# A two-layer decoder step on one core: dense blocks of sample scores, second-layer index keys issued from three queues, page steps at tiles 10 to 44

## What is computed

```
z = rmsnorm(x) @ w_in                                   # 1024 -> 12 pieces: q k v qi ki wi gates, pool, gating
# sample rows: an indexer scores all old keys, 256 of them are attended
score = sum_h relu(qi_h . ki) * wi_h                    # ki: index keys of the pages, 64 wide
idx   = top_k(score, 256)
att   = softmax(q . k[idx]) @ v[idx]                    # k, v: pages of the cache, 512 wide
# prompt rows: the same with their own keys, top 128, causal; besides a pooling and a gating branch
x = x + rmsnorm(concat(branches * silu(gates)) @ w_out)
```

## Time and profile before

| | |
|---|---|
| median of 3 runs | 1106.1 us (1105.05 to 1114.48) |
| the profiled execution's own time | 1108.4 us |
| its span in the trace | 1106.7 us |
| PE busy | 985.8 us, 89% |
| DVE busy | 513.4 us, 46% |
| ACT busy | 322.7 us, 29% |
| pages and index keys, weights and the rest | 205 MB, 185 GB/s on average |

### The profile page before, as it was taken

The page is one execution under the profiler, slowest core; times in us unless marked ns, Lnnn a source line. Parts: engine busy times, 40 slices in busy tenths (PEclk is TensorE's granted clock), DMA queues, the critical chain, the costliest instruction groups (busy, mean ns, idle before and its releaser), DMA issues.

```text
span 1106.7 us, 18204 instructions
## 1 busy us (share of the span) xinstructions
PE 985.8 (89%) x5948; PEld 496.0 (45%) x5948; DVE 513.4 (46%) x1682; ACT 322.7 (29%) x718; POOL 89.3 (8%) x152
## 2 busy tenths in 40 slices
PE   5999987898989999999882999798989899999995
PEld 4534443343434555554451344343434345555542
DVE  4215999335972333232231069983349722332222
ACT  3132312421232544341210321233212324453411
POOL 8300000000000002002110000010000000020000
PEclk9999998898989999999987999998989899999998
DMA  9732657246674847456453224665475746465560
GB/s 299 184 108 77 237 202 286 93 171 237 206 251 157 281 144 256 162 186 216 133 155 111 79 77 154 231 225 208 146 263 173 276 164 247 153 232 192 177 232 29
DMA packets 110019, 205.01 MB, mean 185 GB/s; under 512 B 14439, under 2 KB 29014, under 8 KB 109938
## 3 DMA queue, kind: packets, MB, share of 16 engines
q1 hardware_dynamic: 87186, 141.86, 38.1%
q0 software_dynamic: 17632, 59.99, 15.7%
q10 hardware_dynamic: 5120, 2.10, 0.8%
HBM read 193.87 MB, written 10.14 MB: 184 GB/s over the span
## 4 chain that ended last, share of the span: by engine, by line
PE 60%; DVE 15%; SPq 9%; DMA 8%; issue 4%; ACT 2%; POOL 0%; ACTq 0%; POOLq 0%; DVEq 0%
PE bank L1355 27%; PE bank L1682 9%; DVE r L1006 6%; PE bank L1407 5%; SPq L559 5%; DMA pg<-in_cache_v_dram 3%; DMA pg<-in_cache_k_dram 3%; PE bank L1372 3%; SPq L591 3%; PE bank L1339 2%; PE bank L1611 2%; DMA r<-in_selectors_dram 2%; PE bank L1619 2%; PE bank L1505 2%; PE bank L1575 1%
## 5 line engine op out<-in xcount | busy, mean ns | idle before, releaser
L1355 PE MATMUL bank<-wr,ht 128*128 128x512 f32 (+1 forms) x1024 | 446.8, 591 | 0.9 <-issue 0.6
L1355 PEld LDWEIGHTS bank<-wr,ht 128*128 128x128 f32 x1024 | 194.7, 195 | 222.8 <-issue 208.7
L1006 DVE TENSOR_SCALAR_CACHE_REDUCE r<-r,sel_i 128x1088 bf16<-128x1088 f32 x62 | 82.8, 1335 | 0.0
L1407 PE MATMUL bank<-pg,rs 128*32 128x256 f32 x1024 | 67.0, 401 | 11.7 <-DMA pg<-in_cache_v_dram 11.7
L1339 PE MATMUL bank<-wr,ht 128*64 128x256 f32 (+1 forms) x576 | 68.3, 393 | 5.9 <-ACT r L937 3.4
L1372 PE MATMUL bank<-pg,qbx 128*32 128x256 f32 x1024 | 64.3, 388 | 9.0 <-DMA pg<-in_cache_k_dram 8.0
L1102 DVE CUSTOM_DVE_ANT_0 r<-bank,r 128x256 f32<-128x256 f32 (+2 forms) x48 | 24.9, 555 | 82.1 <-PE bank L1611 82.0
L1682 PE MATMUL bank<-wr,qt 128*128 128x512 f32 x128 | 60.1, 613 | 0.6 <-ACT r L937 0.6
L1682 PE MATMUL bank<-wr,ht 128*128 128x512 f32 x128 | 57.5, 592 | 0.0
L1339 PEld LDWEIGHTS bank<-wr,ht 128*64 128x64 f32 x576 | 42.8, 146 | 28.3 <-ACT r L937 5.1
L1268 DVE MATCH_REPLACE8 r<-m,r 128x256 f32<-128x256 f32 (+2 forms) x96 | 51.1, 542 | 0.0
(11 more groups left out here) (264 smaller groups left out, 1127.8 us busy)
## 6 DMA issues: line engine op xcount, KB each, us to landing
pg<-in_cache_k_dram SPq DMA_DIRECT2D x256, 256.0 KB, 4.3
pg<-in_cache_v_dram SPq DMA_DIRECT2D x256, 256.0 KB, 4.5
wr<-in_w_in_dram POOLq DMA_DIRECT2D x14, 2048.0 KB, 10.0
wr<-in_w_out_dram POOLq DMA_DIRECT2D x4, 2048.0 KB, 9.7
sh<-in_cache_kidx_dram SPq DMA_DIRECT2D x96, 32.0 KB, 4.4
r<-in_x_prompt_dram SPq DMA_DIRECT2D x4, 512.0 KB, 7.0
wr<-in_w_in_dram POOLq DMA_DIRECT2D x2, 1024.0 KB, 9.9
gr<-in_cache_kidx_dram ACTq DMA_DIRECT2D x64, 32.0 KB, 2.6
```

The lines of the kernel that those rows point to most:

```text
L1006: then(nc.vector.tensor_scalar(MSK, SC, scalar, None, ALU.is_ge, ALU.add, accum_out=CNT))
L1355: mm = pe.matmul(b[0:m, 0:w], HT[:, k, rt * P:rt * P + m], W[n % 2][:, k, 0:w], start=(k == 0), stop=(k == KC - 1))
L1407: mm = pe.matmul(acc[r0:r0 + 32, :], RS[n % 2][:, c0:c0 + 32], PG[2 * gi + e][:, g * DP:(g + 1) * DP], start=(j == 0 and u == 0 and e == 0 ...
```

## The change

- `S` and `H` stand in two dense blocks. The first, at the end of tile 7 (second layer: 6), holds `S(0, *)`, `kip`, `H(0)` and `S(1, *)` with no tile between them; the second, a tile later, holds `H(1)`, `S(2, *)`, `wt`, `sgus`, `H(2)`. The search starts there, two tiles earlier in the list.
- One relu of each step stays on ACT, the other goes to DVE, with a semaphore of its own (`s_free1`).
- In the second layer POOL issues the 32 odd keys of pairs 2 and 3 (`pool keys`), between tile 45 and tile 0 of the next layer. SP issues 64 in place of 96.
- The sample tiles of `kg` and `qi` stand at 2 and 3 in the second layer (4 and 5 before), that of `q` at 8 in both (10 before). `T` of `q` and `k` stands two tiles behind its tile in place of one.
- The page steps start at tile 10 in place of 12 and leave out 17, 22 and 27 in place of 15 and 21; the last is at 44 in place of 45. The masks of the first two pairs are split: three pieces at the end of tiles 17 and 18, two pieces, maximum and exponential at the front of 18 and 19.
- The store of the new rows to `x_mid` is issued by ACT in `norm`, ahead of its square, and no longer by POOL.

```diff
 KEY_STEPS = [("keys", 1, pair, j) for pair in (0, 1) for j in range(NCH)]
-
-PLACES = [12, 13, 14, 16, 17, 18, 19, 20, 22, 23, 24, 25] + list(range(26, 46))
+POOL_KEYS = [("pool keys", 1, pair, j) for pair in (2, 3) for j in range(NCH)]
+
+PLACES = [10, 11, 12, 13, 14, 15, 16, 18, 19, 20, 21, 23, 24, 25, 26, 28] + list(range(29, 45))
 PI_PLACES = [(n, part) for n in (18, 19, 20, 21, 22, 23) for part in (0, 2)]
...
-    tiles = [("z", l, "kg", rt) for rt in (RTO if l == 0 else RTP)]
-    tiles[1 if l == 0 else 5:1 if l == 0 else 5] = [("z", l, "qi", ST)]
-    tiles += [("z", l, "qi", rt) for rt in range(PT_TILES)]
-    for name in ("q", "k", "v"):
+    tiles = [("z", l, "kg", rt) for rt in range(PT_TILES)]
+    first = 0 if l == 0 else 2
+    tiles[first:first] = [("z", l, "kg", ST), ("z", l, "qi", ST)]
+    tiles += [("z", l, "qi", 0), ("z", l, "qi", 1), ("z", l, "q", ST), ("z", l, "qi", 2), ("z", l, "qi", 3)]
+    tiles += [("z", l, "q", rt) for rt in range(PT_TILES)]
+    for name in ("k", "v"):
         tiles += [("z", l, name, rt) for rt in RTO]
...
+        put(0, END, POOL_KEYS[7][:1] + POOL_KEYS[7][2:])
...
-    put(9, FRONT, ("kip",))
...
     s0 = 7 if l == 0 else 6
-    put(s0, MID, *[("S", 0, p) for p in range(PAIRS)])
-    put(s0 + 1, MID, ("H", 0), *[("S", 1, p) for p in range(PAIRS)])
-    put(s0 + 2, MID, ("H", 1), *[("S", 2, p) for p in range(PAIRS)])
-    put(s0 + 3, FRONT, ("H", 2))
-    put(s0 + 3, MID, ("wt",))
-    put(s0 + 4, MID, ("sgus",))
+    put(s0, END, *[("S", 0, p) for p in range(PAIRS)], ("kip",), ("H", 0), *[("S", 1, p) for p in range(PAIRS)])
+    put(s0 + 1, END, ("H", 1), *[("S", 2, p) for p in range(PAIRS)], ("wt",), ("sgus",), ("H", 2))
+    put(at["q", ST] + 1, FRONT, ("T", "q", ST))
+    put(at["k", ST] + 2, FRONT, ("T", "k", ST))
     for name in ("q", "k"):
-        for rt in RTO:
-            put(at[name, rt] + 1, FRONT, ("T", name, rt))
+        for rt in range(PT_TILES):
+            put(at[name, rt] + 2, FRONT, ("T", name, rt))
...
     for n, k in enumerate((3, 4, 4, 4, 4, 4, 4, 4)):
-        put(s0 + 3 + n, END, ("srch", a, a + k))
+        put(s0 + 1 + n, END, ("srch", a, a + k))
         a += k
-    put(s0 + 11, FRONT, ("take",))
+    put(s0 + 9, FRONT, ("take",))
...
     put(17, MID, ("snew", 0), ("snew", 1))
-    put(19, END, *[("mk", 0, j) for j in range(NCH + 1)], ("mx", 0), ("exp", 0))
-    put(20, END, *[("mk", 1, j) for j in range(NCH + 1)], ("mx", 1), ("exp", 1))
+    for p in range(2):
+        put(17 + p, END, *[("mk", p, j) for j in range(3)])
+        put(18 + p, FRONT, *[("mk", p, j) for j in range(3, NCH + 1)], ("mx", p), ("exp", p))
...
+        for s, n in zip(POOL_KEYS, (45, 45, 46, 46, 47, 48, 49)):
+            put(n, END, s[:1] + s[2:], layer=l + 1)
...
-                    for par in range(2 if l > 0 and pair >= 2 else 1):
-                        load_keys(sp, mybir.EngineType.SP, l, pair, par, ki_in)
+                    load_keys(sp, mybir.EngineType.SP, l, pair, 0, ki_in)
...
+                elif kind == "pool keys":
+                    pair, j = s[2:]
+                    if j == 0:
+                        keys_free(pool, l, pair)
+                    load_keys(pool, mybir.EngineType.Pool, l, pair, 1, odd_in, (j,))
+                elif kind == "res" and l + 1 == DEPTH:
...
                     act.wait_ge(x_new, done("res", l - 1, rt))
+                    act.dma_start(x_mid[rt * P:rt * P + m, :], X[rt][0:m, :]).then_inc(st_x[rt], 16)
                     act.wait_ge(dve_full, dve_filled("pl", l - 1, 3))
                     act.wait_ge(st_xb, 16 * 9 * l)
                 nc.scalar.activation(JUNK[0:m, :], X[rt][0:m, :], ACT.Square, accum_out=SS[0:m, rt:rt + 1]).then_inc(sq_done, 1)
...
                     act.wait_ge(s_full, done(*s))
-                    for par in range(2):
-                        ins = nc.scalar.activation(RSX[2 * p + par][:, 0:w], bank[4 + 2 * (p % 2) + par][:, 0:w], ACT.Relu)
-                    ins.then_inc(s_free, 1)
+                    nc.scalar.activation(RSX[2 * p][:, 0:w], bank[4 + 2 * (p % 2)][:, 0:w], ACT.Relu).then_inc(s_free, 1)
...
+                elif kind == "S":
+                    j, p = s[2:]
+                    w = 512 if j < 2 else NS
+                    if j == 0 and p == 0 and l > 0:
+                        dve.wait_ge(out_full, l * PAIRS)
+                        dve.wait_ge(act_full, act_filled("out", l - 1, *OUTS[-1]))
+                    if j > 0 and p == 0:
+                        dve.wait_ge(dve_full, dve_filled("H", l, j - 1))
+                    dve.wait_ge(s_full, done(*s))
+                    nc.vector.tensor_scalar(RSX[2 * p + 1][:, 0:w], bank[5 + 2 * (p % 2)][:, 0:w], 0.0, None, ALU.max)\
+                        .then_inc(s_free1, 1)
...
-                    pe.wait_ge(ki_in, 16 * (4 + 6 * l) * NPG)
-                    pe.wait_ge(odd_in, 16 * 2 * NPG)
+                    pe.wait_ge(ki_in, 16 * 4 * (l + 1) * NPG)
+                    pe.wait_ge(odd_in, 16 * 2 * (l + 1) * NPG)
                     pe.wait_ge(act_keys_in, 16 * 2 * (l + 1) * NPG)
...
                 if n >= 2:
                     pe.wait_ge(s_free, n - 1)
+                    pe.wait_ge(s_free1, n - 1)
...
-                        if par == 0:
-                            pe.wait_ge(s_free, done("S", l, j, p))
+                        pe.wait_ge(s_free1 if par else s_free, done("S", l, j, p))
```

More of the change, by code:

```diff
@@ L722, in _ @@
             pool.wait_ge(st_cv, 16 * DEPTH)
+            pool.wait_ge(st_y, 16 * 5)
             for i in range(5):
-                pool.wait_ge(st_x[i], 16 * DEPTH)
+                pool.wait_ge(st_x[i], 16)
         @block.scalar
```

13 lines of the change are left out of this document (5 added, 8 removed).

## The result

The changed kernel takes 1120.95 us (1120.05 to 1122.07), 1.0114 times the kernel before, with a 95% interval of 1.0075 to 1.0152. The forecast was 1106, so it is slower by some 13 us where no change was expected; the range of 8 in 10 ended at 1118. The profiled execution took 1120.7 us, 1119.0 of it span, at a mean granted clock of 0.948 (before 0.956).

The account below looks back on a forecast made before the run. PE was taken as the bound, its longest wait 20.9 us for second-layer index keys. Terms +6 - 11 + 1 + 0 + 2 x 2 = 0 left 1106 us, no change; 8 in 10: 1088 to 1118.

Parts of the forecast that it names:

- Keys: Start of the second layer's scores: PE's 20.9 us wait for index keys goes, 18.0 us gained net of the boundary's cost.
- B: Rival: POOL's key loads push a weight load 11 us late at the layer boundary, 1117 us; chance 0.10.
- C: Rival: the keys stay late because their issue wasn't the limit, 1124 us; chance 0.04.
- Boundary: Between the layers: norms waiting for x_mid stores from ACT, and the sample tile of `kg`, cost +2.9 us (0 to 5).
- Dense blocks and first page steps: Relu waits +1.4 us per layer; page waits 4.0 at `K(0,1)`, 7.4 at `K(1,1)`; with slower clock, page steps cost 15.5.
- rival A: The pages keep up, so first layer -5.5 us and second -9.5, 1091 us; chance 0.25.
- Masks and first V steps: After the first mask product: about 9 us gone and 10 new per layer, +1 in the first, 0 in the second.
- +6: First layer up to its first mask product, put at 177.4: shift of +6 us, pages deciding and not the search.
- The wait at `V(0,3)` moves to `K(2,1)`: Page wait moves to the third pair's key steps, in the same place beside the same weight load: 0 us.
- +2 per layer: Third pair's mask, a tile earlier: PE waits some 4 us for busy DVE, not 0.7, less shorter page waits; 0 to 4.
- +9: Second layer from its scores: +7 us to the first mask product, 0 for masks and V steps, +2 for the third mask.

Follow-up runs that it names:

- b1: The kernel before with one part of the change alone, the second layer's odd keys of the last two pairs issued by POOL: ratio 0.983, 1091.1 us.
- b4_keys_act_stores: b1 with the stores of x_mid issued by ACT in norm and no longer by POOL: ratio 0.982, 1088.9 us.
- a1_pool_stores: The changed kernel with its stores of x_mid on POOL again and POOL's last key steps behind them: ratio 1.012, 1123.4 us.
- d1: b6 with only the first eight page steps moved to the change's tiles, 10 to 16 and 18: ratio 0.998, 1108.0 us.
- b6: The changed kernel with page steps and masks back in the tiles of the kernel before and stores of x_mid on POOL: ratio 0.972, 1077.9 us.
- f2: b6 with only the first eight page steps moved, to tiles 9, 10, 12, 13, 14, 16, 17, 18, leaving gaps: ratio 0.976, 1084.5 us.
- a2: The changed kernel with the third pair's mask and exponentials one tile later, at tile 30 as before: ratio 1.003, 1115.9 us.
- f5: f4 with the third pair's mask at tile 29, ahead of the last pieces of the prompt selection: ratio 1.007, 1118.6 us.
- f1: b6 with the first twelve page steps and the first two masks, split, in the change's tiles: ratio 0.981, 1089.6 us.
- f4: f1 with the third pair's key steps in tiles 24, 25, 26, 28 in place of 26 to 29: ratio 0.998, 1108.0 us.

## Why the prediction was wrong

**Keys: right.** 18.0 us were forecast; b1 gains 18.4 (0.0166 of 1109). Rivals B and C are out: no weight load was late, and no wait for keys is left.

**Boundary: +2.9 was low.** From the sample tile of `out` to the scores the changed kernel takes 63.3 us; before it was 78.9 with the wait of 20.9, so 58.0: +5.3, just above the 0 to 5 given. The part not seen was how late two of the stores land. Of the five in the change, three land after 2.9 to 3.6 us and those of `norm(0)` and `norm(3)` after 8.4 and 8.3, so that DVE waits 5.0 and 6.0 us for them; PE's wait of 7.08 us at 580.42 stands behind the second. That store is issued at 571.20, 2 us behind a weight load of 2 MB; before, it went out at 549.32, 0.9 us ahead of the load, and landed after 3.7. The median hardly moved (3.6 us, before 3.7 for the stores to `x_mid`; the 2.9 of the earlier trace rows has the five last stores of the kernel in it too). b4_keys_act_stores and a1_pool_stores put no price on it that can be measured.

**Dense blocks and first page steps: right within two microseconds, in layer 1.** The forecast had `K(0,1)` waiting 4.0 and `K(1,1)` 7.4; the trace has 3.8 and 5.8 (5.22 above, and 0.59 behind it), and in layer 2 3.2 and 6.0. So rival A is out. From the start of a step to the second half of the next, with a weight load between, had 14.7 and 15.3 us; in the four places of the change it is 13.75 to 14.3. The first mask product was to stand at 177.4 and stands at 176.75. The search, put at 172.1, ended at 176.6. By the earlier trace rows it had taken 89.7 us and not 89.2, and in the change it takes 95.8, since DVE's steps between its pieces wait for PE's tiles (4.2 and 2.1 us). It ended 0.15 us ahead of the first mask product, so that it didn't decide was partly luck. The price of the packed key steps was 15.5 us for each layer, 4 of it clock. d1 against b6 gives it: 140.4 against 124.4 us in layer 1 and 149.4 against 133.7 in layer 2, with a page step (1.93) more done, so 14 us; and d1 against f2 has 4.6 and 5.4 of that as clock.

**Masks and first V steps, +1: low by some 3.** Up to the sample tile of `uv` the layer is 12.1 us behind, with one K step and the new keys more done (1.93 and half of the 0.75 that two take): 9.8, where +7 was forecast (+6 and +1). The two new waits at the prompt scores were to be 2.0 and 1.4 us; they are 2.6 and 2.0.

**The step that failed is everything behind that, in the first layer.** The forecast had "The wait at `V(0,3)` moves to `K(2,1)`, in the same place beside the same load: 0" and "+2 per layer" for the third pair's mask, and no term for the rest. The trace of the change, by its sample tiles against those of before, has +6.4 from `uv` to `xg` and +4.9 from there to `out` (103.6 against 101.3, with a V step and its turning less to do, 2.6): 11.3, where 2 was forecast for both. From `uv` to `xg` PE is idle for 4.1 us more and takes 2.3 more for no more work (clock 0.94 against 0.97). Its waits for the third mask and ahead of the next tile are 3.7 and 3.0 us, where before had 1.4 and 0.4. In the stretch behind it PE waits 1.9 us for the first new rows, since `norm(0)` waits for its store; the forecast had counted only the norms behind it. In layer 2 the same places give 2.6 and 1.8, and that layer came as forecast (+9, measured +8.5). Why the two layers differ stays open, and some of it may be the scatter of single traces. Of the 12.3 us by which the profiled execution is over the forecast, 9.3 lie behind `uv` in the first layer, 2.8 ahead of it and 2.4 at the boundary; the small rest goes the other way.

The third pair's mask was sized too low: it is worth 9 to 10 us in both layers together by the ratios (a2, f5), where 4 was forecast: I had seen DVE's backlog and PE's wait of 3, but not that ACT's copies queue behind the exponential and hold the next tile for another 3, nor the clock. The third pair's key steps, 0 in the forecast, cost 19 us where they are added to f1 (f4). What the forecast said of them did come true: PE waits 3.67 and 0.59 us at `V(0,3)` before, and 2.78 and 1.50 at `K(2,1)` in the change. But that compares one crowded order with another. f1, with the value steps early and no page step in tiles 24 and 25, waits 0.4 us for pages in that stretch. The 19 us are thus no loss against the kernel before, but a gain that this order gave away, and they aren't part of the 11.3.

**The baseline that the sum hid.** The forecast's +6 for the first layer mixed a gain with a loss. b6 shows the blocks and the order worth 12 us (its search ends 16 us sooner than that of before and no longer sets the stage), and the page steps and masks cost 43. Weighed one by one against the same kernel, the case for slower would have been seen to hang on whether the page steps keep pace and the third mask finds DVE free.

## What to carry to other kernels

A double-buffered load has a least distance between steps: here the second half of a step came some 14 us after the start of the step before it, when a weight load went out between them. Packing steps closer than it turns idle slots into waits, and in the one pair of traces compared each microsecond of them came with 0.7 more at a lower granted clock. Before steps are moved earlier, look whether the slots being closed were the gaps in which a transfer hid: the same eight steps, with all later steps left in place, cost 28 us without gaps and 4 with them. Split a bundle of edits in the working before summing it: this one held 30 us of gain (keys and blocks) and 43 us of loss, and a sum near zero says nothing about either; b6_keys_dense_blocks, which keeps only the first, runs at 0.972.

## What the runs showed of the hardware

- The granted clock after short waits: in the change, 2.95 us of waiting ahead of a tile are followed by 10.03 us for the 16 products that take 7.13 at full clock (the rows at 328.34, and the earlier trace rows at 95.72). In the kernel before, the tile at that place took 9.25, so only part of this is the new wait's. In the stretch of d1 above, 6.6 us more idle time came with 4.6 us more of busy time for the same 730 matmuls.
- A store of 512 KB issued by ScalarE lands after 2.9 us at best in the change, and after 2.6, twice, in b4_keys_act_stores; GpSimd's to `x_mid` take 2.9 at best in the kernel before and in b1_keys_only. By the Trainium skill (DMA: Bandwidth & Descriptors, Specifications) the first byte comes 0.4 us sooner from the scalar path; the 0.3 us between 2.6 and 2.9 agree with that about, and the time of the kernel shows none of it.
